# Tokens laid out as the even ones and then the odd ones, with the dilated groups' attention kept within each half

## The reference, cut to what matters

```python
DILATED_GROUPS = ((128, 1), (512, 4), (2048, 16))   # window, dilation
# query t of a group attends to t, t-d, t-2d, ..., t-window
scores = q . k * hd ** -0.5;  m = max(scores);  e = exp(scores - m);  den = sum(e)
o = sum(e * v) / den;         lse = m + log(den)
o = sum over the groups of softmax(lse)[g] * o[g]
```

## Time and profile before

| | |
|---|---|
| median of 3 executions | 953.67 us (953.62 to 955.32) |
| the profiled execution's own time | 954.01 us |
| its span, from first to last instruction | 952.1 us |
| PE busy | 941.4 us, 99% of the span |
| DVE busy | 638.0 us, 67% |
| ACT busy | 423.8 us, 45% |
| mean granted TensorE clock | 0.996 |
| one head of stage A (heads 1 to 7) | 71.07 us |

### The profile page before, as it was taken

The page is one execution under the profiler, slowest core; times in us unless marked ns, Lnnn a source line. Parts: engine busy times, 40 slices in busy tenths (PEclk is TensorE's granted clock), DMA queues, the critical chain, the costliest instruction groups (busy, mean ns, idle before and its releaser), DMA issues.

```text
span 952.1 us, 15052 instructions
## 1 busy us (share of the span) xinstructions
PE 941.4 (99%) x5392; PEld 837.2 (88%) x5392; DVE 638.0 (67%) x1010; ACT 423.8 (45%) x600; POOL 0.2 (0%) x4
## 2 busy tenths in 40 slices
PE   8999999999999999999999999999999999999997
PEld 6898998998998998998998999888888888888886
DVE  7767667567567567567567568666666666566866
ACT  7454354354354354354354355544445444443340
POOL 0000000000000000000000000000000000000000
PEclk9999999999999999999999999999999999999998
DMA  9744545545544544544545546655455554556432
GB/s 345 262 177 177 177 177 177 179 173 176 182 171 176 182 170 176 186 167 176 190 162 179 192 157 235 213 183 208 176 178 196 183 191 176 193 198 273 177 133 89
DMA packets 26680, 178.30 MB, mean 187 GB/s; under 512 B 3359, under 2 KB 3615, under 8 KB 6047
## 3 DMA queue, kind: packets, MB, share of 16 engines
q1 hardware_dynamic: 26208, 173.79, 50.5%
q10 hardware_dynamic: 452, 4.24, 1.1%
HBM read 175.92 MB, written 2.10 MB: 187 GB/s over the span
## 4 chain that ended last, share of the span: by engine, by line
PE 97%; DMA 1%; SPq 1%; DVE 0%; issue 0%; ACT 0%; DVEq 0%
PE proj_ps L342 40%; PE proj_ps L343 20%; PE attn_ps L342 6%; PE attn_ps L336 4%; PE attn_ps L338 4%; PE attn_ps L337 4%; PE attn_ps L343 3%; PE value_ps L336 3%; PE value_ps L338 3%; PE value_ps L337 3%; DMA w_raw<-in_weights 1%; PE mixed_ps L336 1%; PE mixed_ps L338 1%; PE mixed_ps L337 1%; PE mixed_ps L450 1%; PE attn_ps L411 1%
## 5 line engine op out<-in xcount | busy, mean ns | idle before, releaser
L342 PE MATMUL proj_ps<-xt,w_hi 128*128 128x512 f32 x1664 | 582.9, 396 | 2.2 <-DVE qk_f L744 2.2
L343 PE MATMUL proj_ps<-xt,w_lo 128*128 128x256 f32 x1664 | 463.0, 278 | 0.0
L730 DVE TENSOR_TENSOR w_lo<-w_raw,w_hi 128x1024 fp32r<-128x1024 f32 x316 | 371.7, 1220 | 73.3 <-ACT w_hi L576 71.9
L342 PEld LDWEIGHTS proj_ps<-xt,w_hi 128*128 128x128 f32 x1664 | 312.2, 188 | 75.9 <-DVE qk_f L744 2.5
L576 ACT ACTIVATE w_hi<-w_raw 128x1024 fp32r<-128x1024 f32 x316 | 316.3, 1051 | 46.1 <-PE mixed_ps L338 26.3
L343 PEld LDWEIGHTS proj_ps<-xt,w_lo 128*128 128x128 f32 x1664 | 313.0, 188 | 0.0
L595 ACT ACTIVATE corr<-proj_ps 128x256 f32<-128x256 f32 x104 | 39.9, 384 | 289.4 <-PE proj_ps L343 289.4
L744 DVE TENSOR_TENSOR qk_f<-proj_ps,corr 128x256 f32<-128x256 f32 x48 | 20.3, 424 | 77.9 <-ACT corr L595 77.8
L342 PE MATMUL attn_ps<-ya,w_hi 128*128 128x512 f32 x128 | 45.3, 393 | 0.0
L342 PE MATMUL attn_ps<-yp,w_hi 128*128 128x512 f32 x128 | 45.1, 392 | 0.0
L337 PE MATMUL attn_ps<-w_lo,xt 128*128 128x384 f32 x128 | 42.8, 335 | 0.0
(11 more groups left out here) (162 smaller groups left out, 911.4 us busy)
## 6 DMA issues: line engine op xcount, KB each, us to landing
w_raw<-in_weights SPq DMA_DIRECT2D x158, 1024.0 KB, 4.8
first_raw<-in_first SPq DMA_DIRECT2D x8, 512.0 KB, 7.5
res<-in_x_rows ACTq DMA_DIRECT2D x1, 2048.0 KB
out_rows<-res SPq DMA_DIRECT2D x8, 256.0 KB, 2.1
w_raw<-in_weights SPq DMA_DIRECT2D x2, 512.0 KB, 11.5
gamma<-in_gamma_row ACTq DMA_DIRECT2D x1, 1024.0 KB
beta<-in_beta_row ACTq DMA_DIRECT2D x1, 1024.0 KB
mask<-in_mask SPq DMA_DIRECT2D x1, 576.0 KB, 6.0
```

Source lines behind the costliest of these rows:

```text
L342: mm(bank, w_hi[:, slot, cols], tile.rearrange("p a s -> p (a s)"), start=first, stop=False)
L343: return mm(bank[:, SEQ:2 * SEQ], w_lo[:, slot, cols], tile[:, 0, :], start=False, stop=last)
L730: tt(w_lo[:, slot, cols], w_raw[:, slot, cols], w_hi[:, slot, cols].bitcast(F32), ALU.subtract).then_inc(lo_split, 1)
```

## The change

The host puts the tokens in another order: the 128 even ones, then the 128 odd ones (`TOKENS`), for the input, the residual and the mask, and puts the output rows back. In this order token tile 0 is the even tokens and tile 1 the odd ones.

Scores: for the two dilated groups each tile of queries is multiplied with the keys of its own tile alone (256 and 128 columns, four times in a head); for the group with window 128 every query needs both tiles of keys (three matmuls of 256 columns, twice). 14 matmuls in place of 15. Probabilities are 2 rows of 512 in place of one of 384 and one of 768. There are 8 transposes in place of 9, into two PSUM banks; the split of the transposed probabilities is two instructions of 128x512 in place of three of 128x384, on ACT and on DVE. Mix: 512 and 256 columns twice for the first group; 256 and 128 columns twice for each of the others, 12 matmuls as before. The pooling needs tokens in order, so `u_pad` is written with a stride of two elements, and `p_hi` and `p_lo` are made from a read with that stride. The maximum is taken in four instructions with an accumulator in place of three, and one masked addition of 128x512 takes the place of two of 256 and 128 columns.

```diff
 def scores(i):
     pe.wait_ge(qk_split, i * (2 * GROUPS) + 2 * GROUPS)
-    pe.wait_ge(pt_split, FROM + i * GROUPS)
-    q = slice(0, P)
-    for g in range(GROUPS):
-        out = (attn_ps[:, 0:512] if g < 2 else attn_ps[:, THIRD:THIRD + 2 * P]).rearrange(
-            "p (a c) -> p a c", a=2)
-        cols = slice(g * P, (g + 1) * P) if g < 2 else q
-        mm(out[:, :, cols], q_hi[:, g, q], keys[:, g, :, 0:P], start=True, stop=False)
-        mm(out[:, 1, cols], q_lo[:, g, q], keys[:, g, 0, 0:P], start=False, stop=True)
-    q = slice(P, SEQ)
-    for g in range(GROUPS):
-        at = 512 + g * SEQ
-        done = product(attn_ps[:, at:at + SEQ], q_hi[:, g, q], q_lo[:, g, q],
-                       keys[:, g, 0, :], keys[:, g, 1, :])
+    pe.wait_ge(pt_split, FROM + i * PT_BANKS)
+    for t in range(TT):
+        q = slice(t * P, (t + 1) * P)
+        out = attn_ps[:, t * 512:(t + 1) * 512].rearrange("p (a c) -> p a c", a=2)
+        for g in range(1, GROUPS):
+            cols = slice((g - 1) * P, g * P)
+            mm(out[:, :, cols], q_hi[:, g, q], keys[:, g, :, q], start=True, stop=False)
+            mm(out[:, 1, cols], q_lo[:, g, q], keys[:, g, 0, q], start=False, stop=True)
+    for t in range(TT):
+        q = slice(t * P, (t + 1) * P)
+        done = product(attn_ps[:, 1024 + t * SEQ:1024 + (t + 1) * SEQ], q_hi[:, 0, q], q_lo[:, 0, q],
+                       keys[:, 0, 0, :], keys[:, 0, 1, :])
     done.then_inc(scores_ready, 1)
...
 def turn_probs(i):
     pe.wait_ge(probs_ready, i * 2 + 2)
-    for g in range(GROUPS):
-        at = g * 512
-        turn(attn_ps[:, at:at + P], s_sb[:, g * P:(g + 1) * P], ident[:, :])
-        for kt in range(2):
-            src = S0 + g * SEQ + kt * P
-            done = turn(attn_ps[:, at + P + kt * P:at + 2 * P + kt * P],
-                        s_sb[:, src:src + P], ident[:, :])
-        done.then_inc(pt_ready, 1)
+    for kt in range(TT):
+        for t in range(TT):
+            done = turn(attn_ps[:, kt * SEQ + t * P:kt * SEQ + (t + 1) * P],
+                        s_sb[:, t, kt * P:(kt + 1) * P], ident[:, :])
+    done.then_inc(pt_ready, 1)
+    for g in range(1, GROUPS):
+        for t in range(TT):
+            done = turn(attn_ps[:, g * SEQ + SEQ + t * P:g * SEQ + SEQ + (t + 1) * P],
+                        s_sb[:, t, (g + 1) * P:(g + 2) * P], ident[:, :])
+    done.then_inc(pt_ready, 1)
...
 def mix(i):
         for kt in range(TT):
-            queries, cols = ((slice(0, SEQ), slice(0, SEQ)), (slice(P, SEQ), slice(SEQ, PTW)))[kt]
-            mm(out[:, :, queries], v_hi[:, kt, v], pt[:, g, :, cols],
+            if g == 0:
+                queries, bank, cols = slice(0, SEQ), 0, slice(kt * SEQ, (kt + 1) * SEQ)
+            else:
+                queries, bank = slice(kt * P, (kt + 1) * P), 1
+                cols = slice((g - 1) * SEQ + kt * P, (g - 1) * SEQ + (kt + 1) * P)
+            mm(out[:, :, queries], v_hi[:, kt, v], pt[:, bank, :, cols],
                start=(g == 0 and kt == 0), stop=False)
-            done = mm(out[:, 1, queries], v_lo[:, kt, v], pt[:, g, 0, cols],
+            done = mm(out[:, 1, queries], v_lo[:, kt, v], pt[:, bank, 0, cols],
                       start=False, stop=(g == GROUPS - 1 and kt == TT - 1))
...
 def masked_max(i):
-    chain.add(tt(s_sb[:, 0:2 * P], attn_ps[:, 2 * P:4 * P], mask[:, 0:2 * P], ALU.add))
-    chain.link(tt(s_sb[:, 2 * P:S0], attn_ps[:, THIRD + P:THIRD + 2 * P], mask[:, 2 * P:S0], ALU.add))
+    chain.add(tt(s_sb[:, :, SEQ:KEYS],
+                 attn_ps[:, 0:1024].rearrange("p (t c) -> p t c", t=TT)[:, :, SEQ:2 * SEQ],
+                 mask[:, :, SEQ:KEYS], ALU.add))
+    for t in range(TT):
+        chain.add(nc.vector.tensor_tensor_reduce(
+            s_sb[:, t, 0:SEQ], attn_ps[:, 1024 + t * SEQ:1024 + (t + 1) * SEQ], mask[:, t, 0:SEQ], 1.0,
+            -3.0e38, ALU.add, ALU.max, smax[:, t:t + 1]))
+    chain.ready()
     chain.add(nc.vector.memset(smax[:, 4:6], 0.0))
-    for n, at, cols, rest in ((0, 0, slice(0, 2 * P), s_sb), (2, THIRD, slice(2 * P, S0), s_sb),
-                              (1, 512, slice(S0, S0 + S1), mask)):
+    for t in range(TT):
         chain.add(nc.vector.tensor_tensor_reduce(
-            s_sb[:, cols], attn_ps[:, at:at + cols.stop - cols.start], rest[:, cols], 1.0,
-            -3.0e38, ALU.add, ALU.max, smax[:, n:n + 1]))
+            s_sb[:, t, SEQ:KEYS], attn_ps[:, t * 512:t * 512 + SEQ], s_sb[:, t, SEQ:KEYS], 1.0,
+            -3.0e38, ALU.add, ALU.max, smax[:, TT + t:TT + t + 1]))
     chain.ready()
...
 def pool(h):
-    chain.link(copy(tile_of(p_hi, h), sum_f[:, :]))
-    tt(tile_of(p_lo, h), sum_f[:, :], tile_of(p_hi, h).bitcast(F32), ALU.subtract).then_inc(pool_split, 1)
+    hi, lo = (tile_of(part, h).rearrange("p (a n) -> p a n", a=TT) for part in (p_hi, p_lo))
+    chain.link(copy(hi, in_halves(sum_f[:, :])))
+    tt(lo, in_halves(sum_f[:, :]), hi.bitcast(F32), ALU.subtract).then_inc(pool_split, 1)
+def in_halves(row):
+    return row.rearrange("p (n a) -> p a n", a=TT)
...
-        halves_summed(u_pad[:, PAD:PAD + SEQ], 0, j, i)
+        dve.wait_ge(act_evac, banked(0, j) + 1 + i * banked_per(0))
+        main, rest = (row.rearrange("p (a n) -> p a n", a=TT)
+                      for row in (proj_ps[:, j % 2, 0:SEQ], corr[:, j % 2, :]))
+        tt(in_halves(u_pad[:, PAD:PAD + SEQ]), main, rest, ALU.add).then_inc(proj_free, 1)
```

More of the change, by code:

```diff
@@ L81 @@
 assert V_FIRST % RING == 0 and GROUPS == RING
[L82 to L86, removed]
+KEYS = SEQ + (GROUPS - 1) * P
+PT_BANKS = 2
 PAD = 16
+assert all(dilation % TT == 0 for _, dilation in DILATED[1:])
+TOKENS = np.arange(SEQ).reshape(P, TT).T.reshape(-1)
 def banked(n, j):
@@ L152, in layer_kernel @@
                     ("v_hi", [TT, GROUPS * P], F32R),
-                    ("v_lo", [TT, GROUPS * P], F32R), ("mask", [S0 + S1], F32),
-                    ("s_sb", [S0 + S1], F32), ("pt", [GROUPS, 2, PTW], F32R),
+                    ("v_lo", [TT, GROUPS * P], F32R), ("mask", [TT, KEYS], F32),
+                    ("s_sb", [TT, KEYS], F32), ("pt", [PT_BANKS, 2, 512], F32R),
                     ("mixed_corr", [SEQ], F32), ("silu_za", [SEQ], F32),
@@ L303, in _ @@
             load(2, RING + 2)
-            for dst, src in ((mask[:, :], mask_d), (inv[:, :, :], inv_d)):
+            for dst, src in ((mask[:, :, :], mask_d), (inv[:, :, :], inv_d)):
                 sp.dma_start(dst, src).then_inc(consts_landed, 16)
@@ L614, in exp_probs @@
                 act.wait_ge(max_ready, i + 1)
-                for t, cols in ((0, slice(0, S0)), (1, slice(S0, S0 + S1))):
-                    activation(s_sb[:, cols], s_sb[:, cols], ACT.Exp, bias=nmax[:, t:t + 1], scale=SCALE,
+                for t in range(TT):
+                    activation(s_sb[:, t, :], s_sb[:, t, :], ACT.Exp, bias=nmax[:, t:t + 1], scale=SCALE,
                                accum_out=den[:, t:t + 1]).then_inc(exp_done, 1)
@@ L629, in head @@
                     if j == PT_SPLIT:
-                        for g in range(GROUPS):
-                            act.wait_ge(pt_ready, i * GROUPS + g + 1)
-                            activation(pt[:, g, 0, :], attn_ps[:, g * 512:g * 512 + PTW],
+                        for b in range(PT_BANKS):
+                            act.wait_ge(pt_ready, i * PT_BANKS + b + 1)
+                            activation(pt[:, b, 0, :], attn_ps[:, b * 512:(b + 1) * 512],
                                        ACT.Copy).then_inc(pt_hi_done, 1)
@@ L798, in normalise @@
                 chain.link(nc.vector.reciprocal(rden[:, 0:2], den[:, 0:2]))
-                for t, cols in ((0, slice(0, S0)), (1, slice(S0, S0 + S1))):
-                    ts(s_sb[:, cols], s_sb[:, cols], rden[:, t:t + 1], None, ALU.mult).then_inc(probs_ready, 1)
+                for t in range(TT):
+                    ts(s_sb[:, t, :], s_sb[:, t, :], rden[:, t:t + 1], None, ALU.mult).then_inc(probs_ready, 1)
             def pool(h):
@@ L835, in head @@
                     if j == PT_SPLIT:
-                        for g in range(GROUPS):
-                            dve.wait_ge(pt_hi_done, i * GROUPS + g + 1)
-                            tt(pt[:, g, 1, :], attn_ps[:, g * 512:g * 512 + PTW],
-                               pt[:, g, 0, :].bitcast(F32), ALU.subtract).then_inc(pt_split, 1)
+                        for b in range(PT_BANKS):
+                            dve.wait_ge(pt_hi_done, i * PT_BANKS + b + 1)
+                            tt(pt[:, b, 1, :], attn_ps[:, b * 512:(b + 1) * 512],
+                               pt[:, b, 0, :].bitcast(F32), ALU.subtract).then_inc(pt_split, 1)
                     if j == Z_POOL:
@@ L1053, in _mask @@
 def _mask():
-    t, s = np.arange(SEQ)[:, None], np.arange(SEQ)[None, :]
-    tiles = []
+    t, s = TOKENS[:, None], TOKENS[None, :]
+    rows = []
     for tile in range(TT):
-        for window, dilation in DILATED:
+        own = slice(tile * P, (tile + 1) * P)
+        parts = []
```

(10 more changed lines are left out.)

7 lines of the change are left out of this document (4 added, 3 removed).

## The result

| | kernel before | changed kernel |
|---|---|---|
| median of 11 executions each | 953.38 us | 956.23 us |
| ratio of the changed kernel to the one before | | 1.003 (95% interval 1.0022 to 1.0038) |
| the profiled execution's own time, span | 954.01, 952.1 | 956.47, 954.7 |
| one head (heads 1 to 7) | 71.07 | 71.38 |

The change makes the kernel 0.3% slower. I had forecast 950.7 us, 0.3% faster, with a range from 949.8 to 952.3.

What follows compares the result with a forecast made beforehand. PE's instruction list was taken to bound the heads; 0.37 us saved a head, 3.0 us in all, took the profiled 954.01 to 951.0, or 950.7 us against the 953.67 median, range 949.8 to 952.3.

Steps and rivals of the forecast that it cites:

- What bounds the kernel: In the heads PE never waits, busy 71.07 of 71.07 us, so its time is its list of instructions.
- The terms of the sum: PE savings per head: scores 0.13, mix 0.13, turns 0.11 us; together 0.37 a head, 3.0 us in all.
- rival (a): Scores, mix, turns: a 128-column matmul costs its columns alone, so gain 3.7 us, 950.0 us; chance 8%.
- rival (b): Scores and mix: small matmuls in closer order cost more than 0.11 us, gain only 1.0 us, 952.6; chance 10%.
- The cover: Softmax on DVE and ACT grows 0.3 us under 5.8 us to spare; pooling strides add 0.1 us; cost zero.
- rival (c): Softmax in every head: DVE becomes late, PE waits at `probs_ready`, about 955.6 us; chance 3%.
- (d): Pooling map or scores: a new PE wait of 0.2 to 0.4 us, 951.1 us; held in the forecast.
- signs of being wrong: Pairs of 256 and 128 columns above 0.25 us or below 0.19, or PE waiting on DVE in the heads.
- The step that failed: PE in the heads: a removed instruction saves its start-to-start cost, as long as no cover is used up.
- A second term put at nothing: Transfers on SP's queue: loads far ahead, mask's transfer 64 KB smaller, cost zero; nothing on the output's transfer.

Runs made afterwards that it cites:

- experiment 1: Kernel before, with only the mix given the changed kernel's column counts (some columns wrong): 957.33 us, ratio 1.004.
- experiment 2: Changed kernel, with only the mix given the column counts of the kernel before (wrong columns in dilated groups): 952.27 us, ratio 0.9987.
- experiment 3: Changed kernel, same twelve mix matmuls reordered so that the second wide pair (512 and 256 columns) is last: 951.41 us, ratio 0.9982 to the kernel before.
- experiment 7: Changed kernel, plus one 128-column transpose into an unused bank behind each head's mix: 951.85 us, ratio 0.9978 to the kernel before.
- experiment 10: Version of experiment 3, with the last pair of each stage B projection chunk turned round (256 columns, then 512): 949.7 us, ratio 0.9958 to the kernel before.
- experiment 11: Version of experiment 3, plus one 128-column transpose behind each stage B projection chunk: 949.99 us, ratio 0.9965 to the kernel before.
- experiment 12: Version of experiment 3, with the last two pairs of each stage B projection chunk turned round: 948.71 us, ratio 0.9947 to the kernel before.
- experiment 13: Kernel before, old token layout, with only the last pair of each stage B projection chunk turned round: 951.82 us, ratio 0.9983.
- experiment 14: Kernel before, old token layout, with the last two pairs of each stage B projection chunk turned round: 950.28 us, ratio 0.9963.

## Why the prediction was wrong

**What bounds the kernel** held for the heads: PE never waits in heads 1 to 7, and every change of their time is in its list of instructions.

**The terms of the sum** held to the hundredth. Read in the prediction's way, the scores take 1.62 us (1.63 forecast), the turns 0.88 (0.87) and the mix 223.19 - 0.23 - 221.35 = 1.61 (1.60); from start to start the three save 2.94 us in all against 3.0. A pair of 256 and 128 columns in the scores costs 0.91 / 4 = 0.227 us, by the rows below (191.77 - 0.12 - 190.74), as forecast. So rival (a), columns alone, and rival (b), dearer small matmuls in close order, are both out. The Trainium skill's "TensorE: Matmul & The Clock Gate", section "Back-to-back issue gap", has 0.081 us for a 128-column matmul. The trace does not agree: 0.11 us. The Trainium skill's "SBUF — State Buffer", section "Door 1: The DMA port swizzle", has non-contiguous PSUM access slow matmuls down. The trace shows none of it for outputs in two runs of 128 columns, two more a head: the pair's 0.227 us less the 0.109 of a transpose of 128 columns leaves 0.118 for the matmul with such an output, and one of 256 columns in a single run takes 0.120.

```profile
190.74 0.28 PE L392 MATMUL attn_ps<-keys,q_hi 128*128 128x256 f32 x1
...
191.60 0.34 PE L336 MATMUL attn_ps<-keys,q_hi 128*128 128x256 f32 x1
191.77 0.28 PE L337 MATMUL attn_ps<-keys,q_hi 128*128 128x256 f32 x1
...
192.36 0.34 PE L336 MATMUL attn_ps<-w_hi,xt 128*128 128x384 f32 x1
```

```profile
221.35 0.39 PE L455 MATMUL mixed_ps<-pt,v_hi 128*128 128x512 f32 x1
...
222.91 0.44 PE L342 MATMUL proj_ps<-xt,w_hi 128*128 128x512 f32 x1
223.19 0.28 PE L343 MATMUL proj_ps<-xt,w_lo 128*128 128x256 f32 x1
```

**The cover** held: the chain of the softmax got shorter by 0.17 us, not longer by 0.3; strides cost nothing; rival (c), a late DVE, did not happen, and neither did (d). The prediction had given 3% to a kernel slower by over 0.2%, all of it to (c); the kernel is slower by 0.3% in another way. None of the signs of being wrong that it names came up either, for they look only at the instructions that change.

**The step that failed** is the sentence that an instruction taken off PE's list "shortens the run by what it costs from start to start". It takes for granted that the other instructions keep their price. I read the 0.346 us of a pair from one stretch of head 2 and called the rest of the list unchanged: "stages B and C keep every instruction of theirs". The price of a pair is 0.347 or 0.353 us, and in stage A the end of the mix in front selects which. The new mix ends in small pairs, and that costs 0.63 us a head on the 96 pairs behind it, more than the 0.37 saved. Experiments 1 and 2 show this in both directions, and 3 and 7 show that the layout's own work does not bring it about. The second price stood in the trace that I had: two gate chunks of stage B take 11.10 us once and 11.30 in 15 other places, 0.1 us for each chunk. One row by stage for stage B would have shown that the same instructions had two costs, and would have made "the rhythm changes" a rival, with about 96 x 0.0063 = 0.6 us a head and 5 us in all as its price.

**A second term put at nothing** is the end of the run. The prediction looks at the transfers only up to the mask's and has no term for the output's, which lands 0.7 us later with the new layout in every trace. In the fast rhythm, too, the change therefore gains 1.8 us and not 3.0 (experiment 3): 0.35 us less in each of seven heads and 0.3 in head 0 make 2.7, and 0.7 in the output's transfer and 0.2 in the first gate chunks are lost. That was found in the traces afterwards and no run tests it.

**What stays open.** Why there are two rhythms, and a rule by which a sequence leads to one. Seen directly before chunks 0 to 5: tails 512, 256, 256, 128 and 512, 256 of the mix lead to the fast one; two or more small pairs at the end lead to the slow one, also with the last pair swapped or its last matmul missing; a transpose leads to the fast one in all its places; one swap early in chunk 0 does nothing, two at its end do. That a wait of varying length in head 0 draws one or the other, and that one swap makes stage B alternate, points to the timing at which the stream is entered; that was not tested by itself.

Theory A is not the whole of it. In stage B pairs of the same shapes, in the same order, change rhythm with no other matmul between. Two gate chunks, a projection chunk and two gate chunks of the kernel before:

```profile
600.50:611.79 11.29, 11.29 (x66) 9.79 (x65) 8.89 (x13) 5.29 (x7) 0.00 (x0) 1.00 0.61 209
611.79:617.34 5.55, 5.55 (x35) 4.88 (x33) 2.99 (x4) 2.80 (x4) 0.00 (x0) 1.00 0.55 192
617.34:628.63 11.29, 11.29 (x66) 9.79 (x65) 7.79 (x11) 5.28 (x7) 0.00 (x0) 1.00 0.52 186
```

The gate chunks take 5.65 us each and the projection chunk 5.55. No projection chunk of any trace takes more than 5.57, whatever stands in front of it. It reads `ya` and `yp` in place of `xt` and writes two banks of `attn_ps` in place of one of `proj_ps`, so the tiles or banks of a stream have a part in its rhythm as well. Experiments 10 to 14 show that they don't fix it for the gate chunks; which of them matters was not tested. The first pair of gate chunks shows that the history reaches further back than the matmuls directly in front: behind the same 48 matmuls of the pooling map it takes 11.10 us with the mix of the kernel before and 11.29 or 11.30 with each other mix, the one of experiment 3 too, unless a transpose stands behind the mix.

## What to carry to other kernels

In a stream bound by TensorE, first check whether the same instructions cost the same everywhere: divide the length of each stage by its number of matmuls. Where two prices turn up with the same clock and no waits, the sequence in front is a parameter to try, and a reordering at no cost (which pair is last, which part first) can be worth more than the work that a rewrite saves. A saving on such an engine is to be measured with two or three orders of the same instructions before the idea is dropped: here the same change is 0.3% slower in one order and 0.2% faster in another. And compare the end of the run, which nothing covers, even where the change does not touch it.

## What was unexpected about the hardware

The pair of a 512-column and a 256-column matmul settles into gaps that repeat every two or four matmuls (346.7 ns a pair) or every six (353.3 ns a pair), at a granted clock of 1.00 in both. In stage A it stays there for the 192 matmuls of six chunks, across their boundaries and semaphore waits that are already met, and can be moved by a transpose of 0.11 us or by turning two pairs round. Over this kernel the slow rhythm costs up to 4.8 us in stage A and 3 us in stage B, 0.8% in all. Other shapes vary less: the pooling map (48 matmuls of 256 columns) took 5.63 to 5.71 us over the kernels. The 66 matmuls of 384 columns of the values took 11.45 us in every trace with the old layout and 11.47 in every one with the new.

The same output transfers of 256 KB take a median of 2.1 us from issue to landing in the four traces with the old layout and 2.5 to 2.7 in the thirteen with the new one.
